# Second block's norm and input products computed inside the first block's stretch, in plain fp32

## The reference

```
h = rmsnorm(x);  z = h @ w_in                  # 1024 -> 1536: xl (512), gl (512), us (512)
xc = causal_conv4(xl);  h_lru = RG-LRU scan(xc, gates from xc @ wa, xc @ wx)
y_lru = h_lru * gelu(gl)
y_ssm: S5 scan over us (32 groups, complex state of 64), gelu, GLU with a 512x512 product
x = x + concat(rmsnorm(y_lru), rmsnorm(y_ssm)) @ w_out
x = x + (silu(h2 @ w_gate) * (h2 @ w_up)) @ w_down,  h2 = rmsnorm(x), width 2816
y = rmsnorm(x)
```

## Time and profile before

| | |
|---|---|
| median of 3 runs | 2329.43 us (2329.09 to 2330.92) |
| profiled execution | 2331.18 us, its span 2329.4 us |
| PE, DVE, ACT, POOL busy | 95%, 66%, 47%, 18% |
| granted TensorE clock, mean | 0.976 |

### The profile page before, as it was taken

The page is one execution under the profiler, slowest core; times in us unless marked ns, Lnnn a source line. Parts: engine busy times, 40 slices in busy tenths (PEclk is TensorE's granted clock), DMA queues, the critical chain, the costliest instruction groups (busy, mean ns, idle before and its releaser), DMA issues.

```text
span 2329.4 us, 30360 instructions
## 1 busy us (share of the span) xinstructions
PE 2205.3 (95%) x11650; PEld 2119.3 (91%) x11650; DVE 1542.1 (66%) x2581; ACT 1090.7 (47%) x1458; POOL 410.2 (18%) x459
## 2 busy tenths in 40 slices
PE   4876799999999999999999999999999999999996
PEld 2555799999999999999999999999999999999996
DVE  8667546578756656875766578766658875665544
ACT  3444434654634455564444664644455563432232
POOL 6433101024011101321010023111102321100001
PEclk9977899999999999999999999999999999999998
DMA  5762333546333545553353655334455643343331
GB/s 171 210 169 77 115 117 115 152 154 191 123 111 117 176 125 162 168 166 109 117 172 106 151 175 174 127 113 141 152 138 156 173 135 109 117 147 109 124 121 58
DMA packets 200527, 322.81 MB, mean 139 GB/s; under 512 B 89088, under 2 KB 131712, under 8 KB 200256
## 3 DMA queue, kind: packets, MB, share of 16 engines
q1 hardware_dynamic: 200256, 320.65, 45.5%
q0 software_dynamic: 128, 0.23, 0.0%
HBM read 296.39 MB, written 26.53 MB: 139 GB/s over the span
## 4 chain that ended last, share of the span: by engine, by line
PE 88%; DVE 5%; POOL 2%; ACT 2%; issue 1%; DMA 1%; SPq 1%; POOLq 0%; DVEq 0%; ACTq 0%
PE acc L814 27%; PE acc L816 27%; PE acc L815 26%; PE acc L879 3%; PE acc L901 1%; POOL tmp L545 1%; PE acc L900 1%; PE acc L910 1%; DVE rstd L1093 1%; PE acc L890 1%; PE acc L872 1%; DVE w_hl L976 1%; DVE s5prod L976 0%; DMA u<-z_dram 0%; DVE act_hl L976 0%
## 5 line engine op out<-in xcount | busy, mean ns | idle before, releaser
L814 PE MATMUL acc<-act_hl,w_hl 128*128 128x416 f32 x2544 | 905.1, 356 | 18.1 <-DVE act_hl L976 18.1
L816 PE MATMUL acc<-act_hl,w_hl 128*128 128x416 f32 x2544 | 895.2, 352 | 0.0
L815 PE MATMUL acc<-act_hl,w_hl 128*128 128x416 f32 x2544 | 892.4, 351 | 0.0
L976 DVE TENSOR_TENSOR w_hl<-w_raw,w_hl 128x1024 fp32r<-128x1024 f32 x428 | 532.0, 1257 | 78.9 <-ACT w_hl L634 77.6
L814 PEld LDWEIGHTS acc<-act_hl,w_hl 128*128 128x128 f32 x2544 | 479.9, 189 | 29.1 <-issue 16.3
L815 PEld LDWEIGHTS acc<-act_hl,w_hl 128*128 128x128 f32 x2544 | 480.0, 189 | 9.7 <-issue 5.0
L634 ACT ACTIVATE w_hl<-w_raw 128x1024 fp32r<-128x1024 f32 x428 | 443.6, 1051 | 78.6 <-DMA w_raw<-in_w_in 43.4
L816 PEld LDWEIGHTS acc<-act_hl,w_hl 128*128 128x128 f32 x2544 | 479.7, 189 | 0.6
L976 DVE TENSOR_TENSOR x_acc<-x_acc,acc 128x416 f32<-128x416 f32 x480 | 272.9, 585 | 199.1 <-PE acc L816 192.3
L545 POOL TENSOR_TENSOR tmp<-tmp 128x416 f32<-128x416 f32 x135 | 168.3, 1246 | 1123.3 <-ACT tmp L642 1113.3
L814 PE MATMUL acc<-ff_hl,w_hl 128*128 128x416 f32 x880 | 312.3, 355 | 14.8 <-DVE x_acc L976 12.0
(11 more groups left out here) (155 smaller groups left out, 1894.2 us busy)
## 6 DMA issues: line engine op xcount, KB each, us to landing
w_raw<-in_w_ffn SPq DMA_DIRECT2D x330, 512.0 KB, 3.7
w_raw<-in_w_in SPq DMA_DIRECT2D x60, 512.0 KB, 3.4
w_raw<-in_w_out SPq DMA_DIRECT2D x40, 512.0 KB, 3.3
s5y<-y_dram SPq DMA_DIRECT2D x80, 256.0 KB, 4.1
s5t<-t_dram SPq DMA_DIRECT2D x64, 162.0 KB, 3.9
s5v<-v_dram SPq DMA_DIRECT2D x80, 128.0 KB, 3.8
x_acc<-in_x SPq DMA_DIRECT2D x4, 1664.0 KB, 7.3
out_y<-x_acc SPq DMA_DIRECT2D x8, 832.0 KB, 6.5
```

What stands on the lines that cost most here:

```text
L814: pe.matmul(out, w(0), x(0), start=first, stop=False)
L815: pe.matmul(out, w(0), x(1), start=False, stop=False)
L816: return pe.matmul(out, w(1), x(0), start=False, stop=last)
L976: return v.tensor_tensor(out, x, y, op)
```

## The change

Block 1's mixer is cut in two. Its load of x, squares, norm, `h1` and the twelve input products leave the FFN of block 0 and stand in `FIRST` among the conv, gate and S5 steps of block 0 (entries with a third number 1). They are made like those of block 0, by eight fp32 matmuls, without splitting weights or rows. The rest of block 1's mixer follows `SECOND`, a list like `MIXER` without those steps; `MIXER` serves the blocks 2 to 4. What the products make is kept in the second half of the idle `act_hl1` (`kept`: gl and xl rows) and in the FFN's buffers (`zs_next`: us rows), from where `xc` (a copy by ACT) brings an xl row to the conv.

The squares of the norms n1 of blocks 0 and 1 are no longer added by POOL: PE multiplies each of the eight rows by ones and sums in PSUM. In all norms ACT now takes the root straight from PSUM (scale and epsilon in the activation) at the norm's own step, and DVE inverts last. `FIRST` has a new order throughout. The load of x for block 1 waits for `pl_done`. Widths are written as functions of the block, all with the old value 416.

```diff
-FIRST = [('x', 0), ('pa', 0), ('sq1', 0), ('sq1', 1), ('sq1', 2), ('sq1', 3), ('tb', 0), ('pq', 0), ('pb', 0), ('n1', 0), ('h1', 0), ...
+FIRST = [('x', 0), ('pa', 0), ('sq1', 0), ('pq', 0), ('pb', 0), ('sq1', 1), ('sq1', 2), ('tb', 0), ('sq1', 3), ('n1', 0), ('h1', 0), ('h1', 1), ('ts', 0), ('tr', 0), ('tt', 0), ('tb', 1), ('h1', 2), ('h1', 3), ('ts', 1), ('us', 0), ('pc', 0), ('tr', 1), ('tb', 2), ('us', 1), ('gl', 0), ('c1', 0), ('tt', 1), ('ck', 0), ('cs', 0), ('c1', 1), ('cs', 1), ('ks', 0), ('c1', 2), ('gl', 1), ('us', 2), ('ck', 1), ('cs', 2), ('c1', 3), ('ck', 2), ('ts', 2), ('ks', 1), ('ks', 2), ('us', 3), ('ck', 3), ('cs', 3), ('bm', 0), ('tr', 2), ('tt', 2), ('zst', 0), ('bm', 1), ('gl', 2), ('xl', 0), ('cv', 0), ('bt', 0), ('bm', 2), ('tb', 3), ('bt', 1), ('bm', 3), ('pl', 0), ('ks', 3), ('vs', 0), ('ts', 3), ('vs', 1), ('bt', 2), ('ga', 0), ('tr', 3), ('kt', 0), ('tt', 3), ('bt', 3), ('vs', 2), ('vs', 3), ('zl', 0), ('x', 0, 1), ('xl', 1), ('s5', 0), ('sq1', 0, 1), ('sq1', 1, 1), ('sq1', 2, 1), ('gl', 3), ('cv', 1), ('sq1', 3, 1), ('n1', 0, 1), ('bx', 0), ('h1', 0, 1), ('ga', 1), ('s5', 1), ('bx', 1), ('h1', 1, 1), ('la', 0), ('xl', 2), ('h1', 2, 1), ('lb', 0), ('h1', 3, 1), ('lc', 0), ('us', 0, 1), ('us', 1, 1), ('ld', 0), ('cv', 2), ('s5', 2), ('s5', 3), ('xl', 3), ('s5', 4), ('s5', 5), ('ld', 1), ('us', 2, 1), ('s5', 6), ('s5', 7), ('cv', 3), ('gl', 0, 1), ('gst', 0), ('ga', 2), ('s5', 8), ('ga', 3), ('s5', 9), ('us', 3, 1), ('gst', 1), ('bx', 2), ('xl', 0, 1), ('gld', 0), ('s5', 10), ('s5', 11), ('gl', 1, 1), ('s5', 12), ('bx', 3), ('s5', 13), ('la', 1), ('zst', 0, 1), ('xl', 1, 1), ('lb', 1), ('s5', 14), ('gld', 1), ('gl', 2, 1), ('wc', 0), ('lc', 1), ('gst', 2), ('wc', 1), ('ld', 2), ('gs', 0), ('gs', 1), ('xl', 2, 1), ('s5', 15), ('s5', 16), ('gld', 2), ('xl', 3, 1), ('s5', 17), ('ld', 3), ('gst', 3), ('nls', 0), ('wc', 2), ('wc', 3), ('gld', 3), ('nls', 1), ('wc', 4), ('gl', 3, 1), ('gs', 2), ('nl', 0), ('gs', 3), ('ml', 0), ('glu', 0), ('ml', 1), ('glu', 1), ('wc', 5), ('oa', 0), ('ns', 0), ('ms', 0), ('oa', 1), ('oa', 2), ('oa', 3), ('ms', 1), ('out', 0), ...
+SECOND = [(26, ('xc', 0)), (26, ('cv', 0)), (27, ('xc', 1)), (27, ('cv', 1)), (27, ('ga', 0)), (27, ('bx', 0)), (27, ('zl', 0)), (28, ('ga', 1)), (29, ('bx', 1)), (29, ('la', 0)), (30, ('lb', 0)), (31, ('s5', 0)), (31, ('lc', 0)), (31, ('xc', 2)), (33, ('s5', 1)), (33, ('ld', 0)), (33, ('ld', 1)), (34, ('cv', 2)), (35, ('xc', 3)), (35, ('s5', 2)), (35, ('s5', 3)), (35, ('cv', 3)), (36, ('s5', 4)), (36, ('ga', 2)), (36, ('bx', 2)), (37, ('ga', 3)), (37, ('bx', 3)), (37, ('s5', 5)), (38, ('la', 1)), ...
-    out = [(kind, 0, j) for kind, j in FIRST] + [("x", 1, 0)]
+    out = [(kind, b[0] if b else 0, j) for kind, j, *b in FIRST]
...
-                out += [(kind, b + 1, j) for at, (kind, j) in MIXER if at == place]
+                out += [(kind, b + 1, j) for at, (kind, j) in (MIXER if b else SECOND) if at == place]
...
-                act.activation(rstd[:], rstd[:], ACT.Sqrt).then_inc(rstd_done, 1)
+            def root(step):
+                bank, tk = wait_m(act, step), width(step[1])
+                act.activation(root_of(step, tk), acc[:, bank, 0:tk], ACT.Sqrt, bias=sm(EPSC), scale=1.0 / (NCH[step[0]] * P))\
+                   .then_inc(m_freed(step), 1)
...
+                elif kind == "xc":
+                    act.wait_ge(conv_done, b * KL + j)
+                    act.activation(xl[:, 3:3 + tk], kept[:, KL + j, 0:tk], ACT.Copy).then_inc(xc_done, 1)
...
+                    if not sums(kind, b):
+                        bank = m_bank(step)
+                        for k in range(KD):
+                            pe.wait_ge(sq_done, SQ_AT[(kind, b)] + k + 1)
+                            ins = pe.matmul(acc[:, bank, 0:tk], ones[:], first_sq(b, k), start=k == 0, stop=k == KD - 1)
...
-                    if b == 0:
+                    if b < 2:
                         for k in range(KD):
                             if j == 0:
-                                pe.wait_ge(h_made, k + 1)
+                                pe.wait_ge(h_made, h_at("h1", b) + k + 1)
...
-                v.tensor_scalar(rstd[:], acc[:, bank, 0:T], 1.0 / (NCH[step[0]] * P), EPS, MUL, ADD).then_inc(m_freed(step), 1)
+            def reciprocal_root(step):
                 wait_evacuated(v, step)
-                v.reciprocal(rstd[:], rstd[:]).then_inc(rec_done, 1)
+                tk = width(step[1])
+                v.reciprocal(root_of(step, tk), root_of(step, tk)).then_inc(rstd_done, 1)
```

More of the change, by code:

```diff
@@ L19 @@
 TB = TP + TS
-NB, T = 5, 416
+NB, T0, T = 5, 416, 416
 LAST = NB - 1
-TPL = SEQ - LAST * T
+TPL = SEQ - T0 - (LAST - 1) * T
 L = 8
@@ L49, with width, cols5, here @@
 RING, LEAD_HI, LEAD_LO = 6, 3, 2
-assert TPL + TS == T and TPL % L == 0
+assert TPL + TS == T and TPL % L == 0 and T0 % L == 0 and T0 <= T
+C50 = T0 // L
+def width(b):
+    return T if b else T0
+def cols5(b):
+    return width(b) // L
+def here(b):
+    return slice(T0 + (b - 1) * T, T0 + b * T) if b else slice(0, T0)
 IN_ORDER = [("us", 0), ("us", 1), ("us", 2), ("us", 3), ("xl", 0), ("xl", 1), ("gl", 0), ("gl", 1),
@@ L98, with raw, split_here @@
 NU = len(SRC)
[L100 to L105, removed]
+EARLY = 4
+def raw(kind, b, j):
+    return kind in ("us", "xl", "gl") and b < 2
+SPLIT = {u: i for i, u in enumerate(u for u, s in enumerate(SRC) if not raw(*s))}
+OWN = list(SPLIT)[:2 + EARLY]
+assert [SRC[u] for u in OWN] == [("glu", 0, 0), ("glu", 0, 1)] + [("out", 0, j) for j in range(EARLY)]
+def split_here(u):
+    return u < NU and u in SPLIT and u not in OWN
 def early(kind, b, j):
@@ L137, with sums @@
 NCH = {"n1": KD, "nl": KL, "ns": KL, "n2": KD, "nf": KD}
+def sums(which, b):
+    return 0 if which == "n1" and b < 2 else NCH[which] - 1
 SQ_AT = {n: sum(NCH[w] for w, _ in NORMS[:i]) for i, n in enumerate(NORMS)}
-SUM_AT = {n: sum(NCH[w] - 1 for w, _ in NORMS[:i]) for i, n in enumerate(NORMS)}
+SUM_AT = {n: sum(sums(*w) for w in NORMS[:i]) for i, n in enumerate(NORMS)}
 NORM_N = {n: i for i, n in enumerate(NORMS)}
+H_AT = {n: i * KD for i, n in enumerate((k, b) for k, b, j in STEPS if k in ("h1", "h2") and j == 0)}
+HL_AT = {n: i * KD for i, n in enumerate(n for n in H_AT if not (n[0] == "h1" and n[1] < 2))}
 def build(nc, a, outs):
@@ L347, in load_x @@
             def load_x(b):
-                sp.dma_start(x_acc[b % 2][:], a["x"][0][:, :, b * T:(b + 1) * T]).then_inc(x_in[b % 2], 16)
+                sp.dma_start(x_acc[b % 2][:], a["x"][0][:, :, here(b)]).then_inc(x_in[b % 2], 16)
             def load_unit(u):
@@ L552, in _ @@
                     for m in (2 * j, 2 * j + 1):
-                        if m:
+                        if m and sums(which, b):
                             sum_up(which, b, m)
@@ L637, in square @@
                 n = SUM_AT[(which, b)]
+                if not sums(which, b):
+                    act.activation(first_sq(b, k), src, ACT.Square).then_inc(sq_done, 1)
+                    return
                 if k >= 2:
@@ L718, in _ @@
-                    for k in H_PARTS[j] if (kind, b) != ("h1", 0) else ():
+                    if (kind, j) == ("h1", 0) and b >= 2:
+                        act.wait_ge(up_full, (b - 1) * NF)
+                    for k in H_PARTS[j] if (kind, b) in HL_AT else ():
                         act.wait_ge(h_made, h_at(kind, b) + k + 1)
-                        act.activation(act_hl[b % 2][:, 0, k, :], tmp[:, 4 + k % 2, :], ACT.Copy).then_inc(h_hi, 1)
+                        act.activation(act_hl[b % 2][:, 0, k, 0:tk], tmp[:, 4 + k % 2, 0:tk], ACT.Copy).then_inc(h_hi, 1)
@@ L1196, in _ @@
                     v.wait_ge(rstd_done, n + 1)
-                    if (kind, b) == ("h1", 0):
+                    if (kind, b) not in HL_AT:
                         for k in H_PARTS[j]:
-                            stt(rows[:, k, :], x_acc[0][:, k, :], v1(gain + k), rstd[:], MUL, MUL)\
+                            stt(rows(b)[:, k, 0:tk], x_acc[b][:, k, 0:tk], v1(gain + k), root_of(("n1", b, 0), tk), MUL, MUL)\
                                 .then_inc(h_made, 1)
```

285 lines of the change are left out of this document (159 added, 126 removed).

## The result

The changed kernel takes 2337.70 us (median of 7 runs, 2335.14 to 2340.85), the kernel before 2329.09 (7 runs on the same chip, 2326.71 to 2330.92): a ratio of 1.0039, interval 1.0028 to 1.005. The forecast was 2317 us with a range to 2335. In the profiled executions the spans are 2336.3 and 2329.4 us, so 6.9 of the 8.6 us are there to be read.

What follows compares the result with a forecast made beforehand. PE was taken to bound the FFN stretches, chains over several engines the time before the first gate. Terms -53.5 + 8 + 33.4 - 0.6 = -12.7 us gave 2317 us as a median, range 2299 to 2335.

Steps and rivals of the forecast that it cites:

- The other norms: Norms in the stream and at the end: no weight copies late behind ACT's wait, 0.6 us saved at the very end.
- Taken out of the stream: Block 0's FFN: 53.5 us of PE work removed, 8 us of new waits on DVE added, so 45.5 us gained.
- The wait behind the conv: Place 27 of SECOND, block 0's FFN: PE waits 1.9 us while DVE does conv and weight subtraction before adding dn.
- POOL's part: At `s5` 4 in block 0's FFN, now one place behind `s5` 2 and 3: PE waits 3 us for POOL.
- the `xc` copies: Four copies on ACT in block 0's FFN, costed at nothing because ACT is half idle (49.7 of 95 us).
- The 0.1835 us: Time per matmul in the FFN stretches, from 109 in 20 us; prices the twelve removed products at 52.8 us.
- The start, s5 and the tail: Block 0: first product 3.9 us earlier, `s5` 0 at 114.5, last `s5` at 237.5, first gate at 309.5, 33.4 later.
- the rows of block 1: Between `s5` 0 and the last s5: block 1's serial norm chain leaves PE idle 8 us, elsewhere 4 us.
- The second rival: Nothing hides in block 0 because of PE's strict order: +26.4 us, 2343; decided by last `s5` after about 250; chance 0.15.
- The Trainium skill's rule on the shared port: VectorE and GpSimd share a port pair as an exclusive lock, blocking the loser; prediction counted nothing, expecting products to cover it.
- the 17 us: Lengthening of block 0 if each of sixteen s5p pairs on the path paid for the VectorE-GpSimd port lock.
- the third: DVE becomes the bound of block 0's emptied FFN: twelve dn places cost 23 us instead of 8, 2332; chance 0.12.

Runs made afterwards that it cites:

- a_pad160: Changed kernel with 160 unused bytes ahead of u5, putting act_hl at 160 modulo 256 as in the kernel before: 2321.76 us (ratio 0.9966).
- a_oldnorm: a_pad160 with the old form of every norm (VectorE scales and inverts, ScalarE takes the root at the step using it): 2326.25 us (0.9984).
- a_mixnorm: a_pad160 with the new norm form only in block 0, block 1's first norm and the last norm, the old elsewhere: 2320.13 us (0.9956).
- a_pad32: Changed kernel with 32 unused bytes put in ahead of u5: 2336.64 us (ratio 1.0029).

## Why the prediction was wrong

**The direction failed on a step that the prediction did not cost: it took the blocks behind the change to be unchanged.** "The other norms" was its only line on them, at nothing but 0.6 us. They lost 20.7 us of the profile:

- *The spacing of the matmuls*, about 11 us of them. From the first mark to the last there are 5,904 matmuls on `act_hl` and 2,208 on `ff_hl`; 5,904 x 1.2 ns + 2,208 x 2.2 ns = 11.9 us. Shown by a_pad160, in which it is undone: its stretch between these marks is 15.8 us shorter, and 5.1 of them are the clock. Over the whole kernel (7,344 and 2,640) the same differences make 14.6 us; the profiles of the changed kernel and a_pad160 differ by 14.9 us, but as 3.4 of these are the clock, the close agreement is partly luck.
- *The form of the norm*, 5.4 us: three times 1.8 between `nl` and `ns`. The prediction said that behind ScalarE's wait "stand weight copies that lead by three units of 4.4 us; none late". One was late by 1.5 us in each block. Shown by a_oldnorm and a_mixnorm.
- *TensorE's clock*, 5.1 us between the marks of blocks 3 and 4, where 9.5 us are lost for 2.3 to 5.1 in the others. That stops of 2 us can do this is shown; that these two stretches came from the stops ahead of them (1.47 and 1.53 us) is not shown. a_oldnorm and a_mixnorm have no stop for `w_hl` there and lack the second stretch, but so does a_pad160, which has the stop; and of the stops of the same length in blocks 2 and 3 the changed kernel's were followed by no loss, while two of a_pad32's were followed by 1.7 us each.

The three sizes add up to 22.4 us, 1.7 more than was lost.

**Taken out of the stream.** The sum was -53.5 + 8. Measured -41.4. The sum of the waits is nearly as forecast; this is the whole list for 300 to 680 us, where 5.5 of the first row is the first gate's own wait:

```profile
PE acc L899 <- DVE act_hl L1069: 6.1, 2, 5.5
PE acc L899 <- DVE x_acc L1069: 5.5, 5, 2.2
PE acc L1003 <- ACT u L850: 2.2, 1, 2.2
PE acc L899 <- DVE w_hl L1069: 1.5, 1, 1.5
PE acc L993 <- POOL carry L659: 1.1, 1, 1.1
PE acc L965 <- POOL tmp L622: 0.3, 1, 0.3
```

That is 11.2 us against 3.1 before: 8.1 more, forecast 8. That the sum fits is in part luck. The wait behind the conv (forecast 1.9 us) is there, 2.16 us at 428; POOL's part cost 1.1 us for 3; and the waits for `u` (2.2) and `w_hl` (1.5) were not in the list. For `u` the prediction had put the `xc` copies at nothing because ScalarE is half idle. In ScalarE's timeline one of them waits 5.1 us for the conv and holds up what stands behind it, a table load of 1.28 us and then the copy to `u` (read from the timeline; no run takes it away):

```profile
471.99 0.55 ACT L810 ACTIVATE xl<-kept 128x416 f32<-128x416 f32 x1 [5.14 <-DVE tmp L1072]
472.56 1.28 ACT L850 ACT_TABLE_LOAD   x1
```

What was missing is again the clock (3.4 us from 474 on) and the spacing (1,200 x 1.2 + 432 x 2.2 ns = 2.4 us). The 0.1835 us that I took from 20 us of the earlier trace rows was low as well, as a window also counts the matmuls under way at its start, two of the 109: over 200 us it is 200/1067 = 0.1875, so the twelve products were worth 54.0 us, not 52.8. Together -53.5 - 1.2 + 8.1 + 3.4 + 2.4 = -40.8, 0.6 us from what was measured.

**The start, s5 and the tail** were right in mechanism and in size to 5 us: 1.1, 1.8, 4.9 and 4.5 us early at the four marks, so +28.9 for +33.4. TensorE's first product started 4.9 us sooner than before, and the products covered the s5 waits: from `s5` 0 to the last `s5` output TensorE waits 3.8 us where 12 were forecast, 0.3 of them for the rows of block 1, for which 8 were. The second rival, in which they don't, was wrong, as its point of decision (250 us) was not reached.

**The Trainium skill's rule on the shared port** ("SBUF — State Buffer", section "SBUF: two separate sides") was rightly left out of the sum. The slowest s5p between 110 and 235 us, in GpSimd's timeline,

```profile
228.02 1.05 POOL L648 TENSOR_TENSOR s5p<-s5w,s5t 128x216 f32<-128x216 f32 x1 [14.13 <-DVE s5w L1247]
```

takes 1.05 us, four others do too, the other eleven 0.64 or 0.65; none has the 1.70 us of the earlier trace rows. The kernel before had already paid in block 0, with 1.68 us twice and 1.05 four times, so the 17 us were too many in any case. Its reading of the earlier trace rows was wrong in one point: beside the s5p of 0.65 us VectorE was not free but made products from a PSUM bank and a table; beside that of 1.70 us it subtracted weights, with both inputs in SBUF:

```profile
126.71 0.55 DVE L976 TENSOR_TENSOR s5prod<-acc,s5t 128x104 f32<-128x104 f32 x2
...
484.07 1.23 DVE L976 TENSOR_TENSOR w_hl<-w_raw,w_hl 128x1024 fp32r<-128x1024 f32 x1
```

No experiment tested the rule.

**The rivals on either side** came nearer to the time than the forecast, each for a wrong reason: the second (2343) is 5.3 us off, and its mechanism did not occur; the third (VectorE as bound, 2332) is 5.7 us off, and the x_acc waits are 5.5 us, not 23.

The account against the forecast of -12.7: block 0 -4.5, block 0's FFN +4.1, blocks 1 to 4 +20.7, the end -0.7; that is +6.9, as the spans say.

## What to carry to other kernels

Before costing what a change does to the schedule, see which buffers it moves: where the layout is one running sum, a small buffer that changes its place shifts all behind it, and one line of padding, put in before two schedules are compared, puts them back. In a dense stream like this kernel's last FFN, price a stop of TensorE by its length up to about 1 us, at 2 us by its length and a half again; take neither for stretches of small matmuls, where a stop of 0.77 us was followed by the lower clock.
